# First norm reduced into token columns, and an MLP whose down products stream the weights, block by block beside the up products

## The reference

```python
def rms_norm(x, g):
    y = xf * lax.rsqrt(jnp.mean(xf * xf, axis=-1, keepdims=True) + EPS)
    return (y * g).astype(x.dtype)

# block 1: x = x + conv_mixers(rms_norm(x, norm_mix_g), ...); cross attention; PEER expert FFN
# block 2: attention, then
h2 = rmsnorm(x, pre_norm_mlp)                       # 256 x 1024
y = jnp.square(jax.nn.relu(h2 @ w_up)) @ w_down     # 1024 -> 4096 -> 1024
x = x + rmsnorm(y, post_norm_mlp)
```

## Time and profile before

| what | value |
|---|---|
| time, median of 3 runs | 1460.01 us (1459.88 to 1461.21) |
| time of the profiled execution | 1455.57 us |
| its span | 1453.7 us |
| TensorE busy | 1315.1 us, 90% of the span |
| VectorE, ScalarE, GpSimd busy | 958.2, 494.4, 503.2 us |
| HBM over the span | 273 GB/s on average; 426 to 428 GB/s while expert rows are gathered |
| chain that ended last | PE 54%, DMA 21%, DVE 13% |

### The profile page before, as it was taken

The page is one execution under the profiler, slowest core; times in us unless marked ns, Lnnn a source line. Parts: engine busy times, 40 slices in busy tenths (PEclk is TensorE's granted clock), DMA queues, the critical chain, the costliest instruction groups (busy, mean ns, idle before and its releaser), DMA issues.

```text
span 1453.7 us, 25674 instructions
## 1 busy us (share of the span) xinstructions
PE 1315.1 (90%) x9952; PEld 1252.8 (86%) x9952; DVE 958.2 (66%) x2108; ACT 494.4 (34%) x966; POOL 503.2 (35%) x334
## 2 busy tenths in 40 slices
PE   6999999999999887887878787888999999989997
PEld 5999999988889887887868786888886889989997
DVE  4678987765685675859595868655426447683674
ACT  5633456344133121212112121211225455444341
POOL 1578822000225554554545454546012000022220
PEclk9999999999999999898999998989999999999998
DMA  6555555553489999999999999999930125345450
GB/s 247 215 179 195 178 174 175 174 189 123 178 362 392 426 427 428 427 427 428 427 427 426 426 426 427 427 428 427 382 145 29 59 87 178 112 173 202 150 196 35
DMA packets 58090, 397.43 MB, mean 273 GB/s; under 512 B 6288, under 2 KB 9872, under 8 KB 10384
## 3 DMA queue, kind: packets, MB, share of 16 engines
q0 software_dynamic: 36864, 268.45, 44.0%
q1 hardware_dynamic: 21136, 127.76, 24.8%
HBM read 395.14 MB, written 1.05 MB: 273 GB/s over the span
## 4 chain that ended last, share of the span: by engine, by line
PE 54%; DMA 21%; DVE 13%; issue 7%; ACT 4%; POOL 1%; DVEq 0%; POOLq 0%; ACTq 0%
DMA rows_late<-peer_uv_dram,stage 21%; PE bank L721 10%; PE bank L723 10%; PE bank L722 10%; PE bank L970 7%; PE bank L689 6%; PE bank L707 5%; DVE rows_late L1996 3%; ACT w_hi L1175 2%; DVE w_lo L524 1%; PE bank L843 1%; POOL rows_late L631 1%; PE bank L867 1%; DVE probs L1922 1%; DVE probs L1920 1%
## 5 line engine op out<-in xcount | busy, mean ns | idle before, releaser
L970 PE MATMUL bank<-h_norm,rows_late 128*128 128x128 f32 x2816 | 328.7, 280 | 25.4 <-ACT h_norm L1362 25.4
L970 PEld LDWEIGHTS bank<-h_norm,rows_late 128*128 128x128 f32 x2816 | 324.6, 196 | 28.4 <-ACT h_norm L1362 28.4
L524 POOL TENSOR_TENSOR w_lo<-raw,w_hi 128x2048 fp32r<-128x2048 f32 x37 | 172.1, 4652 | 387.9 <-ACT w_hi L1175 387.9
L1996 DVE SCALAR_TENSOR_TENSOR rows_late<-rows_late,squares 128x1024 f32<-128x1024 f32 x176 | 213.5, 1229 | 118.3 <-DMA rows_late<-peer_uv_dram,stage 117.6
L631 POOL DMA_INDIRECT rows_late<-peer_uv_dram,stage x165 | 196.5, 1191 | 135.1 <-PE bank L970 99.9
L970 PE MATMUL bank<-h_norm,rows_early 128*128 128x128 f32 x1280 | 174.2, 304 | 74.0 <-ACT h_norm L1362 73.9
L970 PEld LDWEIGHTS bank<-h_norm,rows_early 128*128 128x128 f32 x1280 | 168.8, 217 | 79.9 <-ACT h_norm L1362 79.7
L1175 ACT ACTIVATE w_hi<-raw 128x2048 fp32r<-128x2048 f32 x94 | 178.9, 1904 | 59.8 <-PE bank L723 49.4
L524 DVE TENSOR_TENSOR w_lo<-raw,w_hi 128x2048 fp32r<-128x2048 f32 x57 | 133.1, 2336 | 97.7 <-ACT w_hi L1175 94.2
L721 PE MATMUL bank<-x_hi_a,w_hi 128*128 128x256 f32 x672 | 191.1, 284 | 2.7 <-DVE x_lo_a L1566 1.8
L723 PE MATMUL bank<-x_hi_a,w_lo 128*128 128x256 f32 x672 | 190.3, 283 | 0.0
(11 more groups left out here) (340 smaller groups left out, 2036.8 us busy)
## 6 DMA issues: line engine op xcount, KB each, us to landing
raw<-w_in_dram SPq DMA_DIRECT2D x28, 1024.0 KB, 4.9
raw<-w_up_dram SPq DMA_DIRECT2D x16, 1024.0 KB, 4.7
raw<-w_down_dram SPq DMA_DIRECT2D x16, 1024.0 KB, 4.8
rows_late<-w_in_dram SPq DMA_DIRECT2D x10, 1024.0 KB, 13.1
raw<-w_kv_dram SPq DMA_DIRECT2D x8, 1024.0 KB, 4.7
rows_late<-w_peer_q_dram SPq DMA_DIRECT2D x5, 1024.0 KB, 12.0
raw<-sc_w_out_dram SPq DMA_DIRECT2D x4, 1024.0 KB, 4.8
raw<-cf_w_pw_dram SPq DMA_DIRECT2D x4, 1024.0 KB, 4.8
```

Of the source, the lines that this page charges most:

```text
L524: api.tensor_tensor(ring(w_lo, i), ring(raw, i), ring(w_hi, i).bitcast(F32), ALU.subtract).then_inc(w_lo_ready[LO_BY[i][0]], 1)
L970: mm = nc.tensor.matmul(ct(Y_ACC[c][t // 4], t % 4, P), expert_rows(k)[:, D + t * P:D + (t + 1) * P], ct(diag, k % DIAGS, P), start=False, ...
L1996: w_.scalar_tensor_tensor(out=row, in0=row, scalar=1.0, in1=h_tok[:, c * D:(c + 1) * D], op0=ALU.mult, op1=ALU.mult, accum_out=pre[:, side ...
```

## The change

1. **First norm.** "mix" joins `BY_TOKEN`. DVE adds pairs of squares (four additions in place of seven), TensorE takes each pair sum at once into two columns, `spread` brings the inverse back. `keep_busy` matmuls stand ahead of, between and behind these. The table of the root function is loaded by a dummy root ahead of the squares. SP loads the identity by itself ahead of the first two weight blocks, the remaining constants behind them, and the third weight block ahead of `mem`.
2. **MLP order.** One loop over 16 blocks: up block b, then the down products of block b-2 of the hidden tiles. `w_down` is cut into 16 blocks of 256 rows x 1024 columns. DVE makes all `w_lo` of the MLP; POOL has none.
3. **Down products.** The hidden tile is the stationary side (128 tokens), the weights move with 512 columns. The results lie by token in four banks (`DOWN_ACC`) that gather over the whole MLP; nothing is drained in between.
4. **Residual.** TensorE turns `x_res` into token form by 16 transposes (tiles "xtok") behind up tile 3; they pass through the `ACC` banks, and ACT copies them to `x_tok` behind `hid_hi` of tile 3.
5. **Last norm.** By token, straight from the four banks: ACT squares with a row sum, and takes the root of one column; DVE multiplies with the gain (a row loaded by a broadcast DMA ahead of the first up block), and finishes each quarter of the output by one operation. The output goes out by token in four DMAs.

```diff
-    for half in range(2):
-        add("w_up_2", range(8 * half, 8 * half + 8), "up", 2, "dve", FH * half)
-        add("w_down_2", range(half, 16, 2), "down", 1, ("act", "dve")[half], 8 * half)
+    for b in range(FH):
+        add("w_up_2", [b], "up", 2, "dve", 2 * b)
+        if b == 1:
+            other("xtok", 4, "act")
+        if b:
+            p.append(("w_down_2", b - 1, [], "dve"))
+    p.append(("w_down_2", FH - 1, [], "dve"))
...
-BY_DVE = range(LOAD_OF["k", 0], LOAD_OF["up", 6])
+BY_DVE = range(LOAD_OF["k", 0], len(LOADS))
...
-BY_TOKEN = ("peer", "post_mix", "post_mlp")
+BY_TOKEN = ("mix", "peer", "post_mix")
...
+            sp.dma_start(ident, T["consts"][:, 0:P]).then_inc(ident_landed, 16)
             load(0)
             load(1)
-            sp.dma_start(const[:], T["consts"]).then_inc(const_landed, 16)
+            sp.dma_start(const[:, P:], T["consts"][:, P:]).then_inc(const_landed, 16)
+            load(2)
...
             for i in range(WHOLE.stop, len(LOADS)):
+                if i == LOAD_OF["up", 0]:
+                    sp.wait_ge(acc_ready, TILE_AT["oa", 0] + 1)
+                    sp.dma_start(gain_row[:, 0:D], T["post_gain"].to_broadcast([P, D])).then_inc(gain_landed, 16)
                 load(i)
...
+            pe.wait_ge(filled, 2)
+            keep_busy(10)
             pe.wait_ge(filled, 4)
-            stat_sum("mix")
+            for j in range(DT // 2):
+                pe.wait_ge(summed, j + 1)
+                for c in range(NC):
+                    mm = nc.tensor.matmul(STAT[:, c:c + 1], ct(squares, 2 * j)[:, c * P:(c + 1) * P], mean_d[:, 0:1],
+                                          start=(j == c == 0), stop=(j == DT // 2 - 1 and c == NC - 1))
+                if j == DT // 2 - 1:
+                    mm.then_inc(stat_ready, 1)
+                keep_busy(1 if j < DT // 2 - 1 else 2)
+            pe.wait_ge(ident_landed, 16)
+            spread("mix")
+            keep_busy(1)
...
+            def down(f, c, half, last=False):
+                w = slot("w_down_2", f // 2)
+                at = f % 2 * D + half * 512
+                return three(DOWN_ACC[c][half][:, :], halves("hid", f, slice(c * P, (c + 1) * P)),
+                             [part[:, at:at + 512] for part in w], f == 0, last)
...
+            for n in range(4):
+                c, part = divmod(n, 2)
+                out = open_tile("xtok", n)
+                for j in range(4):
+                    mm = nc.tensor.transpose(out[:, j * P:(j + 1) * P], x_piece(c, 4 * part + j), ident)
+                mm.then_inc(acc_ready, 1)
+            pe.wait_ge(rooted, len(ROOTS))
+            for b in range(2, FH):
+                for f in (2 * b - 4, 2 * b - 3):
+                    for c in range(NC):
+                        for part in range(2):
+                            mm = down(f, c, part)
+                mm.then_inc(down_done, 1)
+                linear("up", range(2 * b, 2 * b + 2), "w_up_2", b, "mlp", DT, 256)
+            for c in range(NC):
+                for part in range(2):
+                    for f in range(2 * FH - 4, 2 * FH):
+                        mm = down(f, c, part, last=f == 2 * FH - 1)
+                    mm.then_inc(down_summed, 1)
...
+            act.wait_ge(filled, 6)
+            s.activation(sink_e[:, 0:1], eps[:, 0:1], ACT.Sqrt)
             square("mix", lambda k: act.wait_ge(x_landed[k // 4], 16), x_res)
...
+            for f in range(2 * FH):
+                act.wait_ge(hid_ready, f + 1)
+                if f >= FH:
+                    act.wait_ge(down_done, (f - FH) // 2 + 1)
+                s.activation(ct(hid_hi, f % FH), ct(hid, f % 4), ACT.Copy).then_inc(x_hi_ready, 1)
+                for n in range(4 if f == 3 else 0):
+                    drain("xtok", n, ct(x_tok, n, 512), width=512)
+                round_to(LOAD_OF["up", 0] + f + 1)
+            for c in range(NC):
+                act.wait_ge(down_summed, 2 * c + 1)
+                s.activation(x_res[:, 0:512], DOWN_ACC[c][0][:, :], ACT.Square,
+                             accum_out=sum_col[:, 2 * c:2 * c + 1]).then_inc(half_squared, 1)
...
+            for f in range(2 * FH):
+                wait_tile(dve, "up", f)
+                if f >= 4:
+                    dve.wait_ge(x_lo_ready, split_count("hid", f - 4))
+                dve.wait_ge(*freed(w_.scalar_tensor_tensor(out=turns[:], in0=acc("up", f), scalar=0.0,
+                                                           in1=rstd[:], op0=ALU.max, op1=ALU.mult)))
+                link(w_.tensor_tensor(ct(hid, f % 4), turns[:], turns[:], ALU.mult), hid_ready)
+                if f:
+                    hid_low(f - 1)
+                subtract_to(LOAD_OF["up", 0] + f + 1)
...
+            for c in range(NC):
+                for half in range(2):
+                    dve.wait_ge((half_squared, y_squared)[half], c + 1)
+                    tok = done(w_.tensor_tensor(ct(y_gained, 2 * c + half, 512), DOWN_ACC[c][half][:, :],
+                                                gain_row[:, half * 512:(half + 1) * 512], ALU.mult), y_scaled)
+                dve.wait_ge(y_rooted, c + 1)
+                link(w_.reciprocal(y_rstd[:, c:c + 1], y_root[:, c:c + 1]))
+                dve.wait_ge(*tok)
+                for half in range(2):
+                    out = ct(x_tok, 2 * c + half, 512)
+                    w_.scalar_tensor_tensor(out=out, in0=ct(y_gained, 2 * c + half, 512), scalar=y_rstd[:, c:c + 1], in1=out,
+                                            op0=ALU.mult, op1=ALU.add).then_inc(out_ready, 1)
```

More of the change, by code:

```diff
@@ L395, in two_blocks @@
         Y_ACC = [psum[5:7], (psum[4], psum[7])]
+        DOWN_ACC = [psum[5:7], (psum[7], psum[4])]
         H_STAT, X_STAT = psum[5], psum[6]
@@ L1592, in freed @@
                 return done(ins, acc_freed["dve"])
-            for k in range(DT):
-                add_to_sum("mix", k)
+            for j in range(DT // 2):
+                dve.wait_ge(squared, square_count("mix", 2 * j + 1))
+                w_.tensor_tensor(ct(squares, 2 * j), ct(squares, 2 * j), ct(squares, 2 * j + 1), ALU.add).then_inc(summed, 1)
             dve.wait_ge(vec_landed, 16)
```

122 lines of the change are left out of this document (56 added, 66 removed).

## The result

| | before | changed |
|---|---|---|
| median of the runs | 1460.01 us (5 runs, 1457.36 to 1461.21) | 1450.99 us (5 runs, 1449.52 to 1452.41) |
| profiled execution, its span | 1455.57, 1453.7 us | 1449.52, 1447.7 us |
| TensorE, VectorE, ScalarE, GpSimd busy | 1315.1, 958.2, 494.4, 503.2 us | 1319.0, 952.2, 493.1, 459.2 us |

The ratio is 0.994, interval 0.9929 to 0.9952: faster by 9.0 us by the medians, 8.8 (7.0 to 10.4) by the ratio. Forecast was 1447.3 us, a gain of 12.7, in a range of 1441.5 to 1453.5.

A forecast was written before the change was run, and what follows sets the result against it. TensorE, busy 90% of the span, was taken as the bound. Gains of 3.8 (start), 3.0 (MLP) and 5.9 (tail) summed to 12.7 us, from 1460.01 to 1447.3 us, range 1441.5 to 1453.5.

The forecast's parts named there:

- Gain 3.0 us: 5.1 less matmul time, 2.1 given back in the pause: MLP products: would end at 1438.4 us against 1441.4, bounds -2.1 and +6.2.
- The start: First norm: first normed tile at 10.15 us instead of 13.99, gain 3.8 us, bounds 2.2 and 5.4.
- the clock: Start: zeros might lift TensorE's clock before the products, worth 1.6 us; counted as nothing, kept as a bound.
- The pause: MLP head: first down product waits until 1269.65 us, a new pause of some 8.6 us, transposes filling 1.8.
- rival C: MLP: wide matmuls cost 0.240 us each and the clock falls in the new pause; 6.7 us lost, 1454.0 us; 19%.
- Down matmuls 0.2267 us: MLP down products: 384 matmuls of 512 columns at 0.2267 us, 87.1 us in place of 92.2.
- Rival B: MLP down products: columns cost only themselves, 0.2133 to 0.216 us a matmul; 3.4 us more gained, 1443.9 us; 13%.
- The round: MLP steady rounds: TensorE sets the pace at 11.2 us, DVE and ACT need 11.0.
- Rival E: MLP rounds: splitting on DVE and ACT falls behind once a step exceeds 5.6 us; 22 us lost, 1470 us; 5%.
- The end of the products: MLP: products end at 1438.4 us against 1441.4, with 1.0 us added for small gaps where rounds meet.
- The tail: Last product to span's end: 6.4 us in place of 12.3, gain 5.9, bounds 5 and 7.
- Rival D: Gathers after the start: running at their own pace, they don't pass the start's gain on; 3.8 us lost, 1451.1 us; 8%.

The follow-up runs named there:

- experiment 6: The changed kernel without any of the matmuls of zeros at the start: 1452.69 us, 0.9953 of before.
- experiment 4: The changed kernel with DVE making `turns` and `hid` of up tile 3 ahead of the split of up block 2: 1446.25 us, 0.9911 of before.
- Experiment 7: The changed kernel with POOL splitting every third up and down block again from up block 4 on: 1456.35 us, 0.9972 of before.
- experiment 1: The kernel before with only the new start (first norm by token, zeros, order of first loads): 1456.41 us, 0.9978 of before.
- experiment 2: The changed kernel with the old start, so the MLP parts alone: 1453.63 us, 0.996 of before.
- experiment 5: The changed kernel with 19 matmuls of zeros in the pause ahead of the first down product: 1448.92 us, 0.9931 of before.
- experiment 3: The changed kernel with the last turn doing hidden tiles 28 and 29 for all banks, then 30 and 31 bank by bank: 1447.55 us, 0.9918 of before.

## Why the prediction was right, and where it was not

**Direction: right; the sum 12.7, measured 9.0.** The profiles have 3.3 us at the start and 4.9 in the MLP, 8.2 together. The start came back as time at the gathers, and the tail too. The products of the MLP did not: "Gain 3.0 us: 5.1 less matmul time, 2.1 given back in the pause" was forecast, and counted from the first `turns` they ended 1.8 us later than before. That is the term which failed, by 4.8 us; its parts follow below. In the profiles the gain comes from the tail and the start alone. (The sum's upper bound there, +6.2, does not follow from its own terms either: 0.2133 a matmul would give 3.0 + 5.2 = 8.2, or 6.4 with a round that DVE and ACT hold at 11.0.)

**The start (3.8 forecast, 3.3 measured): near in the sum, in part by luck, wrong in its steps.** The step that failed: "Its two one-column products take at most what one record of the old sum took, 1.19/2 = 0.6 us". That priced one pair's products alone. TensorE has four pairs of them with zeros between, and at the lower clock one such turn takes 1.28 us (7.80 to 9.08), where the pairs come 0.6 to 0.9 apart. It was 0.9 us behind when the last pair was summed, and took 0.85 for it. The squares' last pair was also later (8.15, not 7.9), and from the root to the first normed tile it took 1.92 us (10.03 to 11.95), not 1.64. First normed tile 11.95 instead of 10.15. What made up for it is the term that I set to nothing and kept as a bound, the clock: the products began with 1.6 us of slow records instead of 3.4 us, and the profile of experiment 6 puts 2.0 us on it. That it came out at 3.3 is the luck of one execution: the same code gave first gathers from 385.05 to 388.26 us, a gain of 1.3 to 4.5.

**The pause (first down product 8.56 us behind the first `turns`, measured 8.78): right.** Its cause too: DVE does `turns` of tile 3 behind `w_lo`, and experiment 4 removes it by that order alone.

**The clock in the pause: the step that I gave to rival C and left out of the sum.** It fell in all five profiles with the empty pause, and cost 2.7 us in this one and 1.5 to 2.3 in the others, where C had 1.6. The row of before that C named showed a fall with TensorE idle, and the forecast itself had an idle TensorE from 1265 to 1269. It should have stood in the sum. C's other half, 0.240 us for a wide matmul, was wrong.

**Down matmuls 0.2267 us: right.** From 1438.90 to 1441.85 us there are 13 of them, 0.2269 apiece. What lies beside the columns is paid once a matmul (0.0133 us at 256 columns, 0.0136 at 512). The Trainium skill (TensorE: Matmul & The Clock Gate, Back-to-back issue gap) gives N/2.4 + 2.5 ns for the gap of a single matmul, 216 ns for 512 columns, and 131 ns for sustained ones; these rows agree with neither, they have 11 ns more than the first. Rival B, which would end there too, is refuted.

**The round (11.2 us, TensorE's; 11.0 of DVE and ACT): right**, 11.22 measured with a step of DVE at 5.38 us. DVE's and ACT's chain is a little faster than forecast (10.8). Rival E, splitting falls behind, did not happen. Its condition, steps longer than 5.6 us, did not come about. Experiment 7 made some of them longer by another cause, POOL's work beside DVE's, and was slower by 5 us.

**The end of the products (177.3 us behind the first `turns` forecast, 182.1 measured): a missing term.** "I add 1.0 for small gaps where rounds meet": the rounds have none, but the last one has a wait of 2.6 us for `hid_lo`. I had worked out DVE's slack within a round, 3 us, where an up block stands between a hidden tile and its use. In the last turn nothing stands between. The 4.8 us over the forecast are 2.7 for the clock and 2.6 for this wait, less some 0.5 that the gaps were over-sized.

**The tail (6.4 forecast, 5.6 measured): mis-sized by 0.8.** From the last operation of DVE (1443.79 + 1.41) to the span's end it is 2.5 us, where I had put 3.0 from a store of 512 KB; the steps of ACT and DVE took 3.1 us instead of 3.35.

**Rival D**, that the whole gain of the start is lost, is refuted by experiment 1.

## What to carry to other kernels

When work of one kind is interleaved with another, price the first and the last turn apart: the slack that a steady round has (here 3 us for a hidden tile) comes from work that isn't there at its ends. An idle stretch of TensorE costs its length and then the slow matmuls behind it, so a forecast pause of some us should carry that term at once; of the two remedies, reordering the waited-for engine won 6.8 us in the profile (4.7 by the medians), and filling the pause with zeros 2.7 up to the fifth `turns`, of which 1.1 were left at the end (2.1 by the medians). And when several parts are changed together, read each stretch against the same stretch of before: here a gain in the tail hid that the stream of products had become longer. And price a chain of small products on a cold TensorE at the low clock and in full number, not as one link.

## What the runs showed of the hardware

A one-column plain matmul is two records; four records (two products) took 0.50 us at the higher and 0.85 us at the lower clock, and sixteen back to back 3.54 us, 0.22 each: at the lower clock one such record takes longer than an fp32r matmul of 256 columns at the higher (0.120).

An empty stretch of 2.6 us near the end was followed by a fall of the clock in four profiles (experiments 2, 5, 6 and 7) and by none in two (the changed kernel, experiment 4), at the same place of the same code. A stretch of 4.7 us was followed by one in all five profiles that had it (the changed kernel, experiments 2, 3, 6 and 7), and cost 1.5 to 2.7 us (the fifth `turns` 18.5 to 19.8 us behind the first, 17.1 where the clock stayed up).

In the view by stretches the granted clock reads 1.00 at the start of a program before its first recorded change, even where matmuls stand at the lower level: in before at 14.6 to 18 us, in experiment 6 (3.54 us for sixteen one-column records), and in experiment 3, where it reads 1.00 with 0.85 us for four one-column records. There, the distance of the records tells the level and the column does not.

A `w_lo` of DVE took 4.67 us beside one of POOL, and 2.29 alone; a `hid` of 0.42 us took 3.16 us at 1303.65 in that same profile.
